# State-space input products in tiles of 64 output rows, and the last output clusters in pairs

## What is computed

```python
def s5_layer(h, ...):
    u, z = jnp.split(rmsnorm(h, g_pre) @ w_in, 2, axis=-1)
    y = s5_ssm(u, ...)           # x = Bbar u;  h_t = Abar h_{t-1} + x_t;  y = Re(C h_t) + D u_t, per group
    y = jax.nn.gelu(y)
    y = y * jax.nn.sigmoid(y @ w_glu + b_glu)
    y = y * jax.nn.silu(z)
    return h + rmsnorm(y @ w_out, g_post)
```

## Time and profile before

| | |
|---|---|
| median of 3 runs | 3145.1 us (3143.59 to 3145.2) |
| span of the profiled execution | 3145.5 us |
| time of that execution outside its span | not listed; the span lies 0.4 us above the median |
| TensorE (PE) products, busy | 3075.0 us (98%) |
| TensorE weight loads (PEld), busy | 2931.5 us (93%) |
| VectorE (DVE), busy | 2404.3 us (76%) |
| ScalarE (ACT), busy | 1529.5 us (49%) |
| mean granted TensorE clock | 0.992 |
| instructions | 61,783 |

### The profile page before, as it was taken

One profiled execution on the slowest core, in us unless ns is written; L12 is line 12 of the kernel. 1 busy time (PEld: TensorE's weight loads), 2 busy tenths in 40 slices (PEclk: granted clock), 3 DMA queues, 4 the chain that ended last, 5 costly groups with the idle time before them and its releaser, 6 DMA issues.

```text
span 3145.5 us, 61783 instructions
## 1 busy us (share of the span) xinstructions
PE 3075.0 (98%) x26577; PEld 2931.5 (93%) x26577; DVE 2404.3 (76%) x2964; ACT 1529.5 (49%) x2232; POOL 0.2 (0%) x4
## 2 busy tenths in 40 slices
PE   5999999999999999999999999999999999999999
PEld 3889999999999988989999999999899999999998
DVE  7898999788888788776887666687688767556764
ACT  2465664343434556666534444445433556434454
POOL 0000000000000000000000000000000000000000
PEclk7999999999999999999999999999999999999999
DMA  9888869999999745665688666895555554654453
GB/s 409 337 301 331 318 254 349 346 334 350 337 339 342 254 163 212 218 225 175 231 298 307 221 223 240 283 303 202 217 181 189 215 190 158 213 179 159 148 188 121
DMA packets 137025, 791.05 MB, mean 251 GB/s; under 512 B 20081, under 2 KB 38641, under 8 KB 46001
## 3 DMA queue, kind: packets, MB, share of 16 engines
q1 hardware_dynamic: 119714, 769.33, 67.2%
q10 hardware_dynamic: 17040, 17.76, 1.6%
HBM read 769.28 MB, written 17.76 MB: 250 GB/s over the span
## 4 chain that ended last, share of the span: by engine, by line
PE 53%; DVE 2%; ACT 1%; issue 0%; ACTq 0%; DVEq 0%
PE bk L436 52%; DVE wl L1649 1%; PE bk L440 0%; ACT wh L949 0%; DVE pr L1649 0%; DVE Hst L1649 0%; DVE xl L1649 0%; DVE ss L1649 0%; DVE qa L1657 0%; DVE p L1649 0%; DVE X L1649 0%; DVE raw L1657 0%; ACT ln L949 0%; DVE hg L1657 0%; ACT rsy L949 0%
## 5 line engine op out<-in xcount | busy, mean ns | idle before, releaser
L1649 DVE TENSOR_TENSOR wl<-raw,wh 128x2048 fp32r<-128x2048 f32 (+1 forms) x481 | 1092.5, 2271 | 321.1 <-ACT wh L949 318.1
L436 PE MATMUL bk<-HX,wh 128*128 128x256 f32 (+1 forms) x8058 | 1105.8, 294 | 1.8 <-ACT wh L949 1.6
L949 ACT ACTIVATE wh<-raw 128x2048 fp32r<-128x2048 f32 x477 | 911.8, 1912 | 351.1 <-PE bk L436 322.7
L436 PEld LDWEIGHTS bk<-HX,wh 128*128 128x128 f32 x8058 | 1022.2, 188 | 53.4 <-ACT wh L949 2.4
L436 PE MATMUL bk<-HX,wl 128*128 128x256 f32 x4560 | 569.0, 277 | 5.2 <-DVE wl L1649 5.2
L436 PEld LDWEIGHTS bk<-HX,wl 128*128 128x128 f32 x4560 | 542.3, 188 | 7.1 <-DVE wl L1649 7.0
L436 PE MATMUL bk<-hb,wh 128*128 128x256 f32 (+1 forms) x3916 | 488.0, 282 | 0.1
L436 PEld LDWEIGHTS bk<-hb,wh 128*128 128x128 f32 x3916 | 468.2, 188 | 8.2 <-issue 0.3
L1657 DVE SCALAR_TENSOR_TENSOR raw<-raw,cb 128x2048 f32<-128x2048 f32 x192 | 437.5, 2283 | 14.8 <-DMA raw<-in_w_ada 14.7
L436 PE MATMUL bk<-hb,wl 128*128 128x256 f32 x2048 | 253.8, 276 | 0.0
L436 PEld LDWEIGHTS bk<-hb,wl 128*128 128x128 f32 x2048 | 242.5, 188 | 0.0
(11 more groups left out here) (313 smaller groups left out, 2584.1 us busy)
## 6 DMA issues: line engine op xcount, KB each, us to landing
raw<-in_w_ada SPq DMA_DIRECT2D x192, 1024.0 KB, 6.9
raw<-in_w_up SPq DMA_DIRECT2D x128, 1024.0 KB, 6.5
raw<-in_w_down SPq DMA_DIRECT2D x128, 1024.0 KB, 5.7
raw<-in_w_in SPq DMA_DIRECT2D x66, 1024.0 KB, 5.3
raw<-in_kv_w SPq DMA_DIRECT2D x33, 1024.0 KB, 4.9
raw<-in_w_out SPq DMA_DIRECT2D x32, 1024.0 KB, 5.4
raw<-in_s_w_in SPq DMA_DIRECT2D x32, 1024.0 KB, 4.9
raw<-in_fox_w_in SPq DMA_DIRECT2D x32, 1024.0 KB, 4.8
```

The source lines that it names most:

```text
L436: return e.matmul(o_, l_, r_, start=start, stop=stop, skip_group_check=True)
L949: return e.activation(o_, i_, f, **kw)
L1649: return e.tensor_tensor(o_, a_, b_, op)
```

## The change

`s5_inputs` takes the two groups of a pair apart. The weights of a matmul are now 32 rows and 64 columns, the output 64 partitions, and each cluster has 64 matmuls (128 records) in place of 32 (64 records); the moving data are the same. `s5_outputs` is split in two functions. The order of the first eight clusters stays; the last eight come in pairs: local part of q, local part of q + 1, state part of q, state part of q + 1.

```diff
                 for ri in range(2):
                     for i in range(4):
-                        for w in range(4):
-                            rows = slice(32 * w, 32 * w + 32)
-                            last = mm(BK[4 + w][:, c0 + 64 * ri:c0 + 64 * ri + 64], PB[q % 3][rows, 3 - i, ri, :],
+                        for w, gh in itertools.product(range(4), range(2)):
+                            rows, g = slice(32 * w, 32 * w + 32), slice(64 * gh, 64 * gh + 64)
+                            last = mm(BK[4 + w][g, c0 + 64 * ri:c0 + 64 * ri + 64], PB[q % 3][rows, 3 - i, ri, g],
                                       U[rows, q, 64 * i:64 * i + 64], i == 0, i == 3)
-                            if ri and i == 3:
+                            if ri and i == 3 and gh:
                                 last.then_inc(s_xq, 1)
                                 release[4 + w] = (s_hx, 4 * q + w + 1)
-            def s5_outputs(q):
-                b = 3 + q % 5
-                bank = claim(b)
-                place = OUT_POS[q // 2]
-                cl = RAW[place % RING][:, :, :].rearrange("p a b -> p (a b)")
+            def s5_local(q):
+                bank = claim(3 + q % 5)
                 e.wait_ge(s_ks, 16)
                 for n in range(3):
                     for w in range(4):
                         rows = slice(32 * w, 32 * w + 32)
                         mm(bank[rows, 64 * n:192], KS[rows, q, n, :], U[rows, q, 0:192 - 64 * n], n == 0, False)
+
+            def s5_outputs(q):
+                b = 3 + q % 5
+                bank = BK[b]
+                place = OUT_POS[q // 2]
+                cl = RAW[place % RING][:, :, :].rearrange("p a b -> p (a b)")
                 e.wait_ge(s_raw[place % RING], 16 * (place // RING + 1))
...
                     if 6 <= n < 14:
+                        s5_local(n - 6)
                         s5_outputs(n - 6)
-                for q in range(8, 16):
+                for q in range(8, 16, 2):
+                    s5_local(q)
+                    s5_local(q + 1)
                     s5_outputs(q)
+                    s5_outputs(q + 1)
```

More of the change, by code:

```diff
@@ L1 @@
+import itertools
 import numpy as np
```

## The result

The changed kernel takes 3167.9 us (median of 4 runs, 3163.4 to 3171.7) against 3145.2 us: ratio 1.0073, 95% interval 1.0061 to 1.0085, some 23 us slower. The prediction was 3140.6 us, within 3136.5 to 3149.0 us.

A forecast was written before the change was run, and what follows sets the result against it. TensorE, 98% busy, was taken as the bound, VectorE close second. Gains of 2.0 us in early inputs, 2.2 us of VectorE waits and 0.3 us in outputs made 4.5 us off: median 3140.6 us, range 3136.5 to 3149.0 us.

The forecast's parts named there:

- the gain of 0.3 us: Last outputs: 77 records behind the last block limit, all state ones, take 1.2 us instead of 1.5 us.
- 1.25 us a cluster: Input products: 128 new records take 1.25 us instead of 1.95 us, 0.70 us saved a cluster.
- 1.04 us, side by side: Input products, a bound: if the eight new tiles work side by side, 128 records take 1.04 us.
- 11.2 us: Input products: 16 clusters at 0.70 us saved each, on TensorE alone.
- in turn: Rival, inputs: halves of a row group alternate, a cluster stays at 1.95 us, kernel near 3147.9 us; chance 0.13.
- record at today's price: Rival, inputs: each record costs as now, a cluster takes 3.9 us, kernel 3176 us; chance 0.10.
- A block there holds some slab time nearly always: Single input clusters between slabs: blocks nearly always include slab time; 0.2 us put for the few that do not.
- the 3.1 us I had put for the arrival: Instruction supply: time taken for one block of 256 instructions standing alone.
- The 2.9 to 3.8 us of the dense outputs: Last outputs: a block costs at least 2.9 us alone, up to 3.8 us in a row.
- 1.9 us of pause for each: Two input pairs: a whole block takes 3.1 us instead of 1.2 us; 0.65 us lost a pair.
- VectorE's share: From 2302.3 to 2382.5 us: six waits for `wh`, 2.2 us, can vanish, so `filled(0)` ends 4.2 us earlier.
- The slower rival: Rival, inputs: TensorE pays for each record as now, 31 us more, 3176 us; chance 0.10.

The follow-up runs named there:

- the last attempt: The changed kernel with new tiles only in clusters 4, 5, 7, 8, 10, 11, 13, 14, old ones elsewhere: 3142.4 against 3145.6 us, ratio 0.9995.
- the shifted kernel: The changed kernel with 41 more TensorE instructions (waits already met) at its very start: 3163.0 us, ratio 1.0055 against the kernel before.

## Why the prediction was wrong

**What bounds the kernel, and what a pause is.** Right: blocks of 256 instructions, the eight packets more, the pauses that grow with pace. Counted through the trace, waits included, TensorE resumes from each of the four "issue" pauses before and the eleven after a whole number of 256 instructions behind the one before it. In the outputs the gain of 0.3 us did not come. The records behind the last limit take 1.25 us instead of 1.48 us, as worked out, but the first limit's pause ends 5.80 us into the outputs instead of 5.55 us.

**Pace.** Taken at 1.25 us a cluster from a row with 8.9 ns a record; measured 1.52 us, 10.8 ns reckoned the same way and 0.15 us beside it. The 8.9 ns were read rightly for the tables, but their form (32 weight columns, 32 moving) is cheaper than the new one, and the entry was put 0.05 us too low. The bound "1.04 us, side by side" was out of reach. So 0.43 us a cluster were to be had, 6.9 us in all, not 11.2 us. The direction was right; the rivals "in turn" and "record at today's price" both fell.

The Trainium skill, TensorE: Matmul & The Clock Gate, section "Wait — 56ns, not 53.3ns?", puts a floor of about 25 ns between the starts of matmuls. The 128 records in 1.52 us disagree for these tiles: each holds a weight load and a product and takes less than half of that.

**"A block there holds some slab time nearly always" is the step that failed first.** I put 0.2 us for the clusters that stand alone; four of them had pauses of 2.3 to 2.6 us. From cluster 6's pause to cluster 9's lie 506 records (16, three slabs of 39, two clusters of 128, and 117), which with a dozen waits are 1,024 instructions, four blocks exactly. Three steps are nearly four blocks: a resonance, so one block in four falls on a cluster again and again, five records further each time. And the slab time that such a block did hold did not help. The one before 2287.92 us began with the 16 `wl` records before the cluster (2281.95 us) and lasted 1.9 + 1.5 us of work, longer than the 3.1 us I had put for the arrival; yet the pause was 2.60 us. So the next block came 6.0 us after this one was entered. The 2.9 to 3.8 us of the dense outputs were no upper bound.

**What the arrival of a block is made of** can be read from the DMA queues in short windows. The first line below is the whole list of queues from 2281.95 to 2285.70 us, the next two are that from 2285.70 to 2286.80 us (packets, MB, share of 16 engines):

```profile
q1 hardware_dynamic: 143, 1.05, 80.6%
...
q8 instruction: 1, 0.02, 5.5%
q1 hardware_dynamic: 1, 0.00, 0.1%
```

A weight load of 1 MB keeps the DMA engines busy for 81% of the time, and the block's packet starts at 2285.74 us, as the load ends and 3.8 us after TensorE entered the block before. It takes 1.0 us, and TensorE resumes 1.2 us after its end. In front of all seven pauses there is one such packet. It starts 2.8, 3.5, 1.2, 3.8, 3.0, 2.6 and 2.1 us after the entry, takes 0.9 to 1.1 us, and TensorE resumes 1.2 to 1.5 us after its end. The 1.2 us belong to the one case in which no other packet moved meanwhile (2256.66 to 2257.86 us); in the six others the DMA engines were busy for 76% or more. So a block came 3.8 us after the entry with the engines idle, and 4.4 to 6.0 us after it beside weight loads. The longest in any kernel here is 7.7 us (the second pause of the last attempt). That the loads hold the packet up is read from these times, and it is not the whole account: in the shifted kernel one packet starts 1.6 us after the entry (2300.40 to 2301.99 us) with the engines 98% busy. No run moved a load to test it.

**The sizes in the pairs.** I put 1.9 us of pause for each, from a block of 3.1 us; 3.7 us and 4.0 us came. The first block took 5.4 us to arrive, and two limits fell into the second pair, with 5.7 and 3.8 us.

**The clock was left out.** No term of the sum and no rival had it, though the clock column stood in every window. The seven pauses were followed by six slabs at the lower clock, which cost 14.5 us, almost as much as the pauses. It was not needed to miss the range: the pauses at full clock (17.7 - 6.9 - 0.8 = 10.0 us) would have put the kernel near 3155 us, over the 3149.0 us of the upper end. The clock made the loss more than twice as large.

**VectorE's share** was never put to the test: TensorE came later than `filled(0)`, and in the last 100 us before it VectorE now waits for ScalarE, which follows TensorE's slabs. In the waits of VectorE after, from 2,298 us to the state part of output 0 (us, times, longest):

```profile
DVE u L1658 <- ACT u L958: 11.1, 3, 4.2
DVE wl L1658 <- ACT wh L958: 8.7, 7, 1.4
```

Before, this was 3.6 us in nearly the same stretch.

**The slower rival** had the right sign and the wrong mechanism: a price of the record. What cost was the supply of records.

## What to carry to other kernels

- Count instructions per microsecond, not only work. A burst of small matmuls that runs at 12 ns a record empties a block of 256 instructions in 1.5 us. The next one came 2.9 us after the entry at the earliest (before, first pause of the last outputs), 3.4 to 4.1 us in rows of dense blocks, and up to 7.7 us beside weight loads. Halving a tile to run faster doubles the instructions; where the product comes out above the supply, the gain turns into pauses.
- Price a pause of TensorE with the clock behind it: 2.3 us of standing cost 5 us here.
- Lay bursts out so that no block of 256 lies in one, and look for a period of the loop that is nearly a whole number of blocks: it makes the accident permanent.

## What the runs showed that was not expected

- The half clock came behind pauses of 2.3 to 3.7 us in the changed kernel, and behind the 1.86 and 2.16 us that lie close together in its second pair; it did not come behind 1.53 us in its outputs nor 2.02 us in the shifted kernel. But with the old tiles in the first four clusters a pause of 2.02 us was followed by it (granted clock 0.50 from 2326.5 to 2329.9 us), so its length alone does not decide. TensorE's 23 `wh` products then took up to 6.67 us in place of 3.98 us (changed kernel). What else decides stays open. The Trainium skill, TensorE: Matmul & The Clock Gate, section "What's actually happening", says that idle stretches bring the array from 2.4 to 1.2 GHz; the trace agrees.
- The Trainium skill, Runtime: NRT & Kernel Launch, Instruction fetch mechanics, calls the crossing of a block limit mostly hidden. Here it is hidden in blocks that hold nothing but slab records, without one "issue" pause, and cost 17.7 us in sixteen clusters of narrow tiles.
- Two halves of a row group, as 32 x 64 tiles, do twice the records in 78% of the time (1.52 against 1.95 us). So they do not take turns at today's price; whether they overlap in time the runs do not show by themselves.
